# A one-core hybrid decoder step: sample rows on four column groups, the first modulation in turned form, the output projection bank by bank, cache copies placed anew

## The reference

```python
sh1, sc1, g1, sh2, sc2, g2 = split(silu(c) @ w_ada + b_ada, 6)      # a vector of 1024 each
h = rms_norm(x, norm_mix) * (1 + sc1) + sh1
qa, ka, va, qb, kb, vb = split(h @ w_in)                            # 8 + 8 heads of 64
oa = stick_breaking(qa, ka, va)      # samples: over 16 pages of 128 cached rows, by page table
ob = dilated_attention(rotary(qb), rotary(kb), vb)                  # samples: over three windows
x = x + g1 * (concat(rms_norm(oa), rms_norm(ob)) @ w_out)
h = rms_norm(x, norm_ffn) * (1 + sc2) + sh2
x = x + g2 * peer(h)   # 8 heads, each the best 16 of 16384 experts: a row of u and v from DRAM each
y = rms_norm(x, norm_final)
```

## Time and profile before

| what | us |
|---|---|
| time, median of 3 runs (lowest, highest) | 1354.66 (1352.45, 1364.06) |
| the profiled execution, its own time | 1354.59 |
| its span, first to last instruction | 1352.9 |
| PE busy (share of the span) | 1062.9 (79%) |
| DVE busy | 791.8 (59%) |
| POOL busy | 425.8 (31%) |
| ACT busy | 374.6 (28%) |

### The profile page before, as it was taken

How to read it: one execution, slowest core, us unless ns; L and a number is a source line. 1 busy time by engine, 2 the same in 40 slices (tenths; PEclk the granted TensorE clock), 3 DMA queues, 4 the chain that set the end, 5 groups by cost and what they waited for, 6 DMA issues and landing times.

```text
span 1352.9 us, 14688 instructions
## 1 busy us (share of the span) xinstructions
PE 1062.9 (79%) x3386; PEld 493.6 (36%) x3386; DVE 791.8 (59%) x1680; ACT 374.6 (28%) x1030; POOL 425.8 (31%) x449
## 2 busy tenths in 40 slices
PE   6899998998456666989987777777767777777775
PEld 2375774443111110658843322333222333232321
DVE  4203888986423321343356777777786777777755
ACT  1201004434110010012233333333344334444323
POOL 1000003020333210000145545554535554555550
PEclk9897999886786776989998999999989999999998
DMA  8999888898699868998579999999999999999995
GB/s 310 426 336 345 284 302 308 319 349 308 206 315 318 288 210 304 360 353 295 218 278 422 422 422 422 421 422 421 422 394 400 422 416 422 422 421 419 422 421 221
DMA packets 87327, 479.80 MB, mean 355 GB/s; under 512 B 11792, under 2 KB 11817, under 8 KB 46076
## 3 DMA queue, kind: packets, MB, share of 16 engines
q0 software_dynamic: 52032, 349.25, 64.7%
q1 hardware_dynamic: 35260, 130.14, 27.1%
HBM read 476.10 MB, written 70.32 MB: 404 GB/s over the span
## 4 chain that ended last, share of the span: by engine, by line
PE 37%; DMA 36%; issue 10%; DVE 8%; ACT 4%; POOL 2%; SPq 2%; POOLq 1%; DVEq 0%; ACTq 0%
DMA R<-in_uv,idst 25%; PE ps L527 13%; PE ps L812 8%; DMA R<-in_sb_v 6%; PE ps L765 4%; DMA R<-in_sb_k 3%; PE ps L489 3%; PE ps L616 2%; POOL R L449 2%; DVE R L1162 1%; DMA R<-out_dil_v_s 1%; PE ps L498 1%; ACT wgt L1071 1%; DVE R L1476 1%; DMA R<-in_uv,idec 1%
## 5 line engine op out<-in xcount | busy, mean ns | idle before, releaser
L812 PE MATMUL ps<-R,diag 128*128 128x512 f32 x1024 | 483.8, 622 | 152.9 <-ACT diag L1090 152.9
L449 POOL DMA_INDIRECT R<-in_uv,idst x256 | 322.7, 1261 | 332.3 <-PE ps L812 256.1
L1476 DVE CUSTOM_DVE_ANT_0 R<-R,H 128x1024 f32<-128x1024 f32 x264 | 318.6, 1223 | 163.8 <-DMA R<-in_uv,idst 153.4
L812 PEld LDWEIGHTS ps<-R,diag 128*128 128x128 f32 x1024 | 193.2, 196 | 443.6 <-ACT diag L1090 238.7
L527 PE MATMUL ps<-R,HT 128*128 128x256 f32 (+1 forms) x768 | 173.0, 385 | 1.0 <-DVE HT L1357 0.3
L381 POOL DMA_DIRECT2D R<-in_wts x44 | 23.4, 532 | 417.0 <-PE ps L527 249.5
L527 PEld LDWEIGHTS ps<-R,HT 128*128 128x128 f32 (+1 forms) x768 | 119.3, 159 | 55.4 <-issue 12.1
L1068 ACT ACTIVATE gel<-dots 128x2 f32<-128x2 f32 x132 | 26.8, 203 | 378.4 <-DVE dots L1476 378.3
L616 PE MATMUL ps<-R,ast 128*32 128x512 f32 x256 | 76.8, 875 | 67.6 <-DMA R<-in_sb_v 65.0
L1162 DVE TENSOR_TENSOR R<-R 128x1024 f32<-128x1024 f32 x64 | 78.2, 1222 | 71.4 <-ACT R L895 57.3
L489 PE MATMUL ps<-R,cT 128*9 128x256 f32 x384 | 94.2, 402 | 0.6 <-ACT bsel L842 0.6
(11 more groups left out here) (236 smaller groups left out, 874.3 us busy)
## 6 DMA issues: line engine op xcount, KB each, us to landing
R<-in_wts POOLq DMA_DIRECT2D x48, 1024.0 KB, 8.3
R<-in_sb_k SPq DMA_DIRECT2D x128, 256.0 KB, 4.9
out_dil_k_s<-in_dil_k SPq DMA_DIRECT2D x32, 1023.5 KB, 8.5
out_dil_v_s<-in_dil_v SPq DMA_DIRECT2D x32, 1023.5 KB, 8.4
R<-in_sb_v SPq DMA_DIRECT2D x64, 256.0 KB, 4.5
R<-in_sb_v POOLq DMA_DIRECT2D x64, 256.0 KB, 4.6
R<-in_uv,idst POOLq DMA_INDIRECT x256, 12.1
m_all<-in_dil_k POOLq DMA_DIRECT2D x16, 192.0 KB, 6.0
```

The lines of the kernel that those rows point to most:

```text
L449: pool.indirect_dma_start(out=R[:, row_slot(k), :], out_offset=None, in_=A["uv"], in_offset=bass.IndirectOffsetOnAxis(ap=idst[:, par, k:k ...
L812: last = pe.matmul(ps[:, banks + q, :], diag[:, k % 4, :], R[:, row_slot(k), D + q * 512:D + (q + 1) * 512], start=False, stop=False, skip ...
L1476: dve.tensor_tensor_reduce(u, u, H[:, t, :], 1.0, 0.0, ALU.mult, ALU.add, dots[:, k:k + 1]).then_inc(s["dot_done"], 1)
```

## The change

- The 8 sample rows are kept as 128 rows of 256 columns (`x4`, `H4`, `s4`, in `G`): four column quarters, 32 partitions each, the prompt's condition row being row 8 of each quarter. A weight piece is now two 128-row blocks of the weights with all 1,024 columns, and PE multiplies 32 columns of the turned rows by each quarter into its own column group (`ada_slots`, `sample_rows`). The bias comes with a DVE add (`ada_rows`), which in the attention of the prompt stands at the end of each pair of heads.
- The condition vectors arrive turned; sigmoid is taken on 128 x 256. The prompt rows are turned right after normalization, and scale and shift are applied to the turned rows, chunk by chunk (`modulate_turned`), from turned vectors. They are no longer spread.
- The projection fills four banks of 512 columns (two tiles, two halves) over four pieces, in three rounds, with evictions per bank; the order of its columns is q, k, q, k, v, v. Queries are spread after the first piece of round 1, from 128 rows.
- The three late vectors are spread between the value windows. Value windows have four buffers; the first two are loaded among the value pages.
- The output projection holds all four pieces and finishes one bank after another, with the sample rows and the first tile's turn between; sums and modulation follow each tile. The weights' slots are released in the fourth bank.
- Copies in SP's list: 16 pieces (samples 0, 1) and two of sample 2 ahead of key page chunk 4, and not before five weight pieces are used; six of sample 2 among the key pages; all eight of sample 3 after value chunk 2 of sample 0; 32 (samples 4 to 7) in the tail.
- The last sample step works on 128 x 256, with sums over the quarters by a matmul, and four output DMAs.

```diff
-QA, KA, VA, QB_, KB_, VB_ = (DG * n for n in range(6))
+QA, KA, QB_, KB_, VA, VB_ = (DG * n for n in range(6))
+ROUNDS = 3
...
-DV = [R[:, 6 + s, 0:3 * DG].rearrange("p (g n) -> p g n", g=3) for s in range(2)]
+DV = [R[:, s, 0:3 * DG].rearrange("p (g n) -> p g n", g=3) for s in (8, 9, 6, 7)]
...
-    sp.dma_start(cwork[0], A["c9"]).then_inc(s["c9_in"], 16)
-    sp.dma_start(const[:, :], A["consts"]).then_inc(s["c_in"], 16)
+    sp.dma_start(cT[:, :, :], A["cT"].rearrange("p (c n) -> p c n", c=KC)).then_inc(s["ct_in"], 16)
+    sp.dma_start(ident, A["consts"][:, 0:P]).then_inc(s["id_in"], 16)
+    for t in range(2):
+        sp.dma_start(x[:, t, :], A["x"][t * P:(t + 1) * P, :]).then_inc(s["x_in"], 16)
+    sp.dma_start(G[:, :, :], A["grp"].rearrange("p (v n) -> p v n", n=WC)).then_inc(s["g_in"], 16)
+    sp.dma_start(const[:, P:], A["consts"][:, P:]).then_inc(s["c_in"], 16)
...
+    def key_pages(b, first=False):
         for c in range(CPB):
-            page_chunk(sp, b, c, A["sb_k"], k_ready, [(s["k_used"], b * CPB + (c - KVS + 1))])
+            page_chunk(sp, b, c, A["sb_k"], k_ready,
+                       [] if first and c < KVS else [(s["k_used"], b * CPB + (c - KVS + 1))])
+            if first and c == KVS - 1:
+                sp.wait_ge(s["w_used"], 5)
+                copy_windows(0, 0)
+                copy_windows(0, 1)
+                for m in range(2):
+                    copy_piece(1, 0, m, 0)
+    key_pages(0, first=True)
+    with sp.Fori(1, NB // 2) as i:
+        for m in range(2):
+            copy_piece(1, 0, m, i)
+            key_pages(i * 2 - 1 + m)
+    key_pages(NB - 1)
...
-    for m in range(2):
-        copy_piece(1, 1, m, 0)
     sp.wait_ge(s["k_used"], NB * CPB)
-    value_pages(0, first=True, q=0)
-    with sp.Fori(1, NB // 2) as i:
-        value_pages(i * 2 - 1)
-        value_pages(i * 2, q=i)
-    value_pages(NB - 1)
-    sp.wait_ge(s["new_out"], 32)
-    sp.wait_ge(s["dk_used"], NB)
+    value_pages(0, (0, 2), first=True)
+    sp.wait_ge(s["new_out"], 64)
     for b in range(2):
         window_rows(sp, DV, b, b, A["dil_v"], A["dil_v_s"], dv_ready)
-    with sp.Fori(1, NB // 2) as i:
-        for j in range(2):
-            sp.wait_ge(s["vd_used"], i * 2 + (j - 1))
-            window_rows(sp, DV, i * 2 + j, j, A["dil_v"], A["dil_v_s"], dv_ready)
-            copy_piece(1, 1, j, i)
+    copy_windows(1, 1)
+    value_pages(0, (4, 6))
+    with sp.Fori(1, NB) as b:
+        value_pages(b, range(0, CPB, 2))
+    sp.wait_ge(s["dk_used"], NB)
...
+    for b in range(2, NB):
+        if b >= 4:
+            sp.wait_ge(s["vd_used"], b - 3)
+        window_rows(sp, DV, b, b % 4, A["dil_v"], A["dil_v_s"], dv_ready)
...
-    for pair, odd in ((2, 1), (3, 0), (3, 1)):
+    for pair, odd in ((2, 0), (2, 1), (3, 0), (3, 1)):
...
+    def ada_slots(r, first, bank, slots):
+        for k in slots:
+            w_round(r + first, k)
+            for c in range(2):
+                for q in range(QUADS):
+                    last = pe.matmul(ps[q * QUAD:(q + 1) * QUAD, bank, 0:WC], cT[:, 2 * k + c, :],
+                                     WA[k][:, c, q * WC:(q + 1) * WC], start=(k + c == 0), stop=(2 * k + c == KC - 1))
+            last.then_inc(s["w_used"], 1)
...
+    def sample_rows(k, bank):
+        for c in range(2):
+            for q in range(QUADS):
+                last = pe.matmul(ps[q * QUAD:(q + 1) * QUAD, bank, 0:WC], hs[:, c, k * QUAD:(k + 1) * QUAD],
+                                 WA[k][:, c, q * WC:(q + 1) * WC], start=(k + c == 0), stop=(2 * k + c == KC - 1))
+        return last
...
+    ada_slots(0, 0, 0, range(WSLOTS))
+    pe.wait_ge(s["c_in"], 16)
+    pe.wait_ge(s["xs_ready"], 1)
+    pe.matmul(ps[:, 2, 256:257], cst("gfold"), stat[:, 3:4], start=True, stop=True).then_inc(s["xs_mm"], 1)
+    pe.wait_ge(s["ada_ev"], 1)
+    turn_group(mq[:, 0, :], 3, 0, s["mt_mm"])
+    ada_slots(1, 0, 1, range(2))
+    pe.wait_ge(s["h_ready"], 3)
+    for t in range(2):
+        turn_prompt(t, (4 + 2 * t, 5 + 2 * t), s["xT_mm"])
+    ada_slots(1, 0, 1, range(2, WSLOTS))
+    pe.wait_ge(s["xT_ev"], 1)
+    turn_group(H4[:, :], 4, 0, s["xT_mm"])
+    pe.wait_ge(s["ada_ev"], 2)
+    turn_group(mq[:, 1, :], 3, 2 * P, s["mt_mm"])
...
+    def qkv_slot(r, k):
+        w_round(r + 2, k)
+        if r == 0:
+            pe.wait_ge(s["hm_ready"], 2 * k + 2)
+        for n in range(4):
+            t, half = divmod(n, 2)
+            if k == 0 and r > 0:
+                pe.wait_ge(s["qkv_ev"], (r - 1) * 5 + n + 1)
+            for c in range(2):
+                last = pe.matmul(ps[:, n, :], hT[:, 2 * k + c, t * P:(t + 1) * P], WA[k][:, c, half * 512:(half + 1) * 512],
+                                 start=(k + c == 0), stop=(2 * k + c == KC - 1))
+            if k == WSLOTS - 1:
+                last.then_inc(s["qkv_mm"], 1)
+        if k == 0:
+            if r == 0:
+                pe.wait_ge(s["hs_ready"], 1)
+            else:
+                pe.wait_ge(s["qkv_ev"], r * 5)
+        sample_rows(k, 4).then_inc(s["w_used"], 1)
+    def query_rows(b, bank, r, mm):
+        for q in range(2):
+            row = q * QUAD + b
+            last = pe.matmul(ps[:, bank, q * WC:(q + 1) * WC], ident[:, row:row + 1].to_broadcast([P, P]),
+                             s4[:, r, :], start=True, stop=True)
+        last.then_inc(mm, 1)
+    for r in range(ROUNDS):
         for k in range(WSLOTS):
-            ada_chunk(r, 0, 0, k, 0)
-    spread_rows((SHIFT1, SCALE1), 0, (4, 5, 6, 7), s["bc_mm"], s["bc_ev"])
-    for k in range(WSLOTS):
-        project(base, 0, k, s["qkv_ev"], k - 1 if k >= 2 else None)
-    for b in range(NB):
-        pe.matmul(ps[:, 4 + b % 4, :], ident[0:NB, b:b + 1].to_broadcast([NB, P]), QKV[0:NB, 2, QA:QA + DG],
-                  start=True, stop=True).then_inc(s["qb_mm"], 1)
-    with pe.Fori(1, QKV_CH // WSLOTS) as r:
-        for k in range(WSLOTS):
-            project(base, r, k, s["qkv_ev"], r * WSLOTS + (k - 1))
+            qkv_slot(r, k)
+            if r == 1 and k == 0:
+                pe.wait_ge(s["qkv_ev"], 5)
+                for b in range(NB):
+                    if b >= 3:
+                        pe.wait_ge(s["qb_ev"], b - 2)
+                    query_rows(b, 5 + b % 3, 0, s["qb_mm"])
...
+        if not first:
+            pe.wait_ge(s["ada_ev"], g + 2)
+        ada_slots(g, 5, 6, range(2))
...
+    for b in range(2, NB):
+        window_pv(b, b % 2, (b // 4 + 1) * 64)
+        pe.wait_ge(s["bc2_ev"], b - 1)
+        spread(LATE + SHIFT2 + (b - 2) // 2, b % 2, 1 + b % 2, s["bc2_mm"])
+        window_row(b - 1, (b - 1) % 2)
+    pe.wait_ge(s["bc2_ev"], 8)
...
+    def out_bank(n):
+        t, half = divmod(n, 2)
+        for c in range(KC):
+            last = pe.matmul(ps[:, n, :], hT[:, c, t * P:(t + 1) * P], WA[c // 2][:, c % 2, half * 512:(half + 1) * 512],
+                             start=(c == 0), stop=(c == KC - 1))
+            if n == 3 and c % 2 and c < KC - 1:
+                last.then_inc(s["w_used"], 1)
+        if n == 3:
+            last.then_inc(s["w_used"], 1)
+        else:
+            last.then_inc(s["out_mm"], 1)
     pe.wait_ge(s["mg_ev"], 4)
     for k in range(WSLOTS):
-        project(ADA_CH + QKV_CH, 0, k, s["out_ev"], k - 1 if k >= 2 else None, late=(k == 0))
-    spread_rows((SHIFT2, SCALE2, GATE2), 2, (4, 5, 6, 7), s["bc2_mm"], s["bc2_ev"])
+        w_round(9, k)
+    out_bank(0)
+    pe.wait_ge(s["ss_ready"], 1)
+    pe.matmul(ps[:, 7, 0:1], cst("hfold"), stat[:, 14:15], start=True, stop=True).then_inc(s["ss_mm"], 1)
+    out_bank(1)
+    pe.wait_ge(s["mg_ready"], 3)
+    turn_group(H4[:, :], 7, 256, s["mg_mm"])
+    out_bank(2)
+    pe.wait_ge(s["mg_ev"], 5)
+    for k in range(WSLOTS):
+        last = sample_rows(k, 6)
+    last.then_inc(s["out_mm"], 1)
+    pe.wait_ge(s["h_ready"], 4)
+    turn_prompt(0, (0, 1), s["hT_mm"])
+    out_bank(3)
+    pe.wait_ge(s["xs_ready"], 2)
+    pe.matmul(ps[:, 4, 0:1], cst("gfold"), stat[:, 3:4], start=True, stop=True).then_inc(s["xs_mm"], 1)
+    pe.wait_ge(s["h_ready"], 5)
+    turn_group(H4[:, :], 7, 0, s["hT_mm"])
+    pe.wait_ge(s["h_ready"], 6)
+    turn_prompt(1, (2, 5), s["hT_mm"])
...
+        dve.tensor_scalar(hT[:, c, 0:SEQ], hT[:, c, 0:SEQ], mT[:, 1, b, at:at + 1], mT[:, 0, b, at:at + 1],
+                          ALU.mult, ALU.add).then_inc(s["hm_ready"], 1)
...
+    def residual(n, mm, wait):
+        t, half = divmod(n, 2)
+        cols = slice(half * 512, (half + 1) * 512)
+        tmp = tw[:, n * 512:(n + 1) * 512]
+        dve.wait_ge(mm, wait)
+        step(dve.tensor_tensor(tmp, ps[:, n, :], m_all[:, GATE1, cols], ALU.mult))
+        dve.tensor_tensor(x[:, t, cols], x[:, t, cols], tmp, ALU.add).then_inc(s["out_ev"], 1)
...
+    step(dve.tensor_tensor(H4[:, :], ps[:, 0, 0:WC], mq[:, LATE + GATE2, :], ALU.mult))
+    step(dve.tensor_tensor(x4, x4, H4[:, :], ALU.add))
+    sample_sum(H4[:, :], 18).then_inc(s["f4_ready"], 1)
+    dve.wait_ge(s["f4_mm"], 1)
```

(1 more changed line is left out.)

621 lines of the change are left out of this document (312 added, 309 removed).

## The result

The changed kernel takes 1295.83 us, the median of 4 runs (1294.31 to 1301.29), against 1353.56 (1351.93 to 1364.06) for the kernel before on the same chip: ratio 0.9565, 95% interval 0.9509 to 0.9621. The profiled execution took 1296.18 us, 58.4 less than the one shown of before. Forecast were 1312 and -42.5. Every term had the right sign; in size only those of the key pages, of the step behind them and of the output stage were near.

The account below looks back on a forecast made before the run. Bounds change by stage: PE until the queries, DVE on key pages, finally the gathers' DMA rate. Terms -10 - 3 + 1.5 - 10 - 6 - 13 + 3 - 5 = -42.5 us from 1354.6 give 1312; own range 1298 to 1326, wide 1284 to 1338.

Parts of the forecast that it names:

- expert queries to the end: Last stage: +3 us for 32 tail copies instead of 24, -5 us for the shorter last sample step.
- I take 0.11: Modulation and sample rows: each new 32-column pass takes 0.11 us, between 0.075 with full overlap and 0.226 with none.
- Page 4 shifts by 12 us, not 24: Key pages: queries are ready 24 us earlier, but page 4, sent behind SP's copies, comes only 12 us earlier.
- my mark of failure: Key pages: a first page wait over 8 us was listed as a sign that the forecast is wrong.
- 1.7 + 9 - 5.3: Key pages behind page 4: +1.7 us bias adds, +9 six copies, -5.3 less copy traffic and PE no longer late.
- Rival 4: Copies hold the pages behind them in SP's queue for their whole 8.6 us landing: slower, 1388 us; chance 0.05.
- 3.5 us: Value pages: each of three samples that lose their two copies gains 3.5 us, -10 together.
- I take 4: Windows: a period with a spread takes 4 us, between 5.1 at low and 3.1 at full clock; stage -6 us.
- nothing in the diff touches that rate: Experts: the gathers' rate stays at 422 GB/s, so only that stage's start and last microseconds can move.
- Rival 1: Passes overlap as in the value pages, clock stays full, DMA gives way: -80 us, 1275 us; chance 0.15.
- Rival 2: DMA bounds everything up to the experts: key pages 0, value pages -7, experts +10, 1332 us; chance 0.21.
- Rival 3: The column groups do not overlap, so the layout does not do what it says: 1325 us; chance 0.07.

Follow-up runs that it names:

- run 2: Changed kernel with the loops over row blocks and column groups exchanged, four passes in a row to one group: 1289.44 us, ratio 0.9511.
- Run 6: Changed kernel with only sample 0's eight copies ahead of key page 4, the other sixteen among the key pages: 1288.92 us, ratio 0.9523.
- run 10: Changed kernel with R, the buffer for pages, weights and gathered rows, as the first tile of all: 1303.77 us, ratio 0.9625.
- run 12: Changed kernel with R as the first tile and sixteen copies spread among the key pages: 1294.49 us, ratio 0.9564.
- run 7: Changed kernel with sample 3's eight copies moved from the first value sample to the tail, behind the value pages: 1306.33 us, ratio 0.9638.
- run 11: Changed kernel with two value buffers for the windows instead of four and the six gate spreads behind the windows: 1297.09 us, ratio 0.9569.
- run 8: Changed kernel with an unused 32-byte tile ahead of R, the buffer for pages, weights and gathered rows: 1304.74 us, ratio 0.9643.
- runs 5: Changed kernel measured once more without an edit, as base for three variants: 1291.19 us, ratio 0.9537.

## Why the prediction was right, and where it was not

By the stages of the two profiled executions, whose differences add to the spans' 58.4:

| stage | forecast | measured |
|---|---|---|
| to the last key page (318.01, 309.46) | -10 | -8.6 |
| to the first value product | -3 | -2.9 |
| first value sample | +1.5 | +4.6 |
| other value samples | -10 | -6.1 |
| windows | -6 | -16.2 |
| output projection to expert queries | -13 | -17.4 |
| expert queries to the end | +3 - 5 | -11.8 |

**Up to the key pages: right in sum, the parts larger.** The projection starts at 41.9 (45 said), the queries are ready at 90.4 (98 said), 31.6 us earlier instead of 24. The step "I take 0.11" a pass was too high: 0.067. I had taken a third of the value pages' pace away (0.075 to 0.11) for the shorter passes; nothing of it was lost, in run 2 neither. A pass of 0.12 is in the trace too, in the first four modulation pieces, each behind a wait of 0.6 to 9.0 us, and 0.114 in the next two:

```profile
17.81 1.94 PE L506 MATMUL ps<-R,cT 128*32 128x256 f32 x16 [3.24 <-DMA R<-in_wts]
...
37.36 1.93 PE L506 MATMUL ps<-R,cT 128*32 128x256 f32 x32
```

16 passes after the wait take as long as 32 without one. The view by windows has 1.00 for the clock at the first of them too, but that is no reading: the trace's records of the clock begin at 36.4 us, and the view counts what lies ahead as full. The 16 passes of the kernel's end take the same 1.93 us, and there the clock is recorded:

```profile
1286.50:1289.50 3.00, 1.93 (x16) 0.59 (x16) 0.88 (x3) 1.49 (x2) 0.00 (x0) 0.50 0.43 175
```

So the first pieces very likely ran at the low clock. It costs little, since they wait for DMA. The spread of the queries (8 said) took 7.17.

**Key pages: right, for a partly right reason.** "Page 4 shifts by 12 us, not 24": DVE's product on it moved from 134.22 to 124.95, 9 us. The last copy was issued at 102.8, earlier than the 115 said, but the pages behind it took 20.7 us to land, where 5.4 is the median of all key pages. So my mark of failure, a first page wait over 8 us, was met by 24.5 us while the stage's end was met within 1.4. What carries the stage's end is the shift of page 4: from DVE's product on it to the end it took 183.8 us before and takes 184.5, so the bias adds, the six copies and the smaller waits behind it came to 0.7 us (1.7 + 9 - 5.3 = 5.4 by the terms, 2 by the -10 that was taken). Whether the long wait is a loss of its own is open. Run 6 took it away and ended the stage at the same time, with the queries 5.2 us later; runs 10 and 12, at the other place of R, say some 9 us for the whole kernel.

**Rival 4** (slower, each copy holding the pages for its landing of 8.6 us) is half in the trace: the two pages of chunk 4 did wait behind copies in SP's queue. But no loss of 8.6 us a copy came with it. Run 6, with sixteen copies among the pages, is not a microsecond later at the keys' end, and run 12 is earlier than run 10. The ring order that the Trainium skill states (DMA: Bandwidth & Descriptors, Queues, rings and completion order) fits the 20.7 us. While page 4 was on its way, from 104.3 to 125 us, the DMA share was 0.99: the engines had other work.

**Value pages: sizes off.** The eight copies ahead of pages 4 and 6 cost the first sample 4.6 us, not 1.5 (run 7 gives 6 for all eight), and the "3.5 us" that a sample gained by losing two copies was nearer to 2. The forecast had read the same rows in two ways: 20 against 17 us a sample gave 1.5 us a copy among the key pages and 3.5 for two among the values.

**Windows: the mis-sized term.** "5.1 us at the low clock, 3.1 at the full one; I take 4." The step that failed is "I take 4". In the timeline the changed kernel has 3.09 us a period with a spread in it, the full clock's value of the sum, so six periods gave 5.5 us more. "The unchanged first two" were not unchanged either, nor the sample row ahead of them:

```profile
506.36 1.88 PE L602 MATMUL ps<-msk,selst 128*8 128x512 f32 x2
508.71 3.11 PE L721 MATMUL ps<-R,ast 128*32 128x512 f32 x12 [0.47 <-ACT selst L942]
...
493.31 0.83 PE L646 MATMUL ps<-msk,selst 128*32 128x256 f32 x4
494.63 1.92 PE L766 MATMUL ps<-R,ast 128*32 128x512 f32 x12 [0.49 <-ACT selst L985]
```

That is 2.2 us. And the six periods of before are 5.3 us apart (515.12 to 541.63 us, 2.2 of it the wait for rows), so that even 4 us a period gave some 8 and not the 6 that went into the sum. Put by causes: the 13.4 us of waits went in full, six spreads came in (1.0 us of PE each), and the clock and the halved rows gave about as much back. The clock's own price is what run 11 shows: 3.2 against 1.92 us a period without a spread, 1.3 x 6 = 8 us. I had given the clock a middle value instead of asking what would hold it up: with the spreads or with the buffers it stays up, each suffices.

**Output stage: right in kind.** 64 passes in 3.66 us (7 said), and 42.3 us for the whole, 47 said. Of the 4.4 us more, 3.3 are the passes.

**The last stage: a cause outside the argument.** The end, from the first of its 16 passes to the last instruction, fell from 16.7 us to 8.0, -8.7 where -5 was said: the passes take 1.93, not a saving of 2.8 but of 6.8, and that at the low clock. The gathers took 264 x 1.05 MB at 427 instead of 422 GB/s, 7.7 us less. What remains of -11.8 is +4.6, which I put down to the eight copies more in the tail; +3 was said, and at 2.43 us each (run 7) their 19.4 us were three quarters covered. The 7.7 us, and some 5 in the earlier stages, are R's place (run 8), by which "nothing in the diff touches that rate" failed: the diff changes sizes of tiles ahead of R. Without that accident the kernel stands at 1304 (runs 8 and 10), 8 us from the forecast. That nearness is in part luck as well: the windows gained 10 us more than said, the value pages 7 less.

**Rivals 1 to 3.** Rival 1 (1275, DMA gives way) had the windows and output terms nearly right and failed at the key pages, where it had -26 and -8.6 came. Rival 2 (DMA the bound up to the experts) had the other value samples right (-7, -6.1 measured) and failed at the key pages (0, -8.6 measured) and at the last stage (+10 - 5, -11.8 measured). Rival 3, as a price, is refuted by the 1.07 us of L536; its reason, that the groups do not overlap, is neither shown nor refuted (run 2). The rule that a change of tiling mode drains TensorE (the Trainium skill, TensorEngine Tiling (Array Packing), Key Properties) would have put a gap around each of the 12 slots; L536 starts at 48.95, before the modelled end of the pass ahead of it, and a slot costs the path 1.0 us. The trace shows no such gap: from 42 to 90 us PE is busy 48.00 of 48.00 us.

## What to carry to other kernels

When a step ahead of a stage with full DMA gets faster by 32 us, as the queries here, the stage need not end 32 us earlier (8.6 here): ask when the first transfer behind the queue's other work can land, and count from there. Copies without a reader belong into stages whose DMA has room (eight of them cost 6 us there and 19 beside the gathers). If the time changes with the size of an unrelated tile, look at where the buffers of the transfers begin, and count from the partition's first byte. And where a term depends on the clock, ask what keeps the engine busy there, instead of taking a value between the two.

## What the runs showed of the hardware

- The place of the receiving buffer moved the gathers between 420 and 427 GB/s and the whole kernel by 13 us (runs 5, 8, 10). The rate was the higher one in all eight traces in which the buffer began on a multiple of 256 bytes, and in none of the six others.
- 16 float32 passes of 256 columns with 32-column weights take 1.07 us, 3.4 times as fast as full-width passes by the column, and 1.09 us with four in a row to one group. Between full and 32-column work no gap is visible.
- A copy from DRAM to DRAM of 1.05 MB beside the gathers cost about as much time as a gather of 1.05 MB into the buffers: 2.43 (one pair of executions) and 2.46 us.
- Two conditions, neither of which alone lowered the granted clock in the window stage (0.95, 0.94), lowered it together (0.73; 0.50 behind a wait of 3.8 us).
- The trace has no record of the clock before 36.4 us; the 1.00 that the view shows there is none.
